# FFN gates through a DRAM scratch, and the adaLN quarters of a group in one burst: a two-layer streaming encoder

## What is computed

```python
def encoder_layer(x, c, ...):
    mod = jax.nn.silu(c) @ w_ada + b_ada
    sh1, sc1, ga1, sh2, sc2, ga2, sh3, sc3, ga3 = [m[:, None, :] for m in jnp.split(mod, 9, axis=-1)]
    h = rms_norm(x, gains[0]) * (1 + sc1) + sh1
    x = x + MACARON_W * ga1 * rms_norm(swiglu(h, w_f1_in, w_f1_out), gains[1])
    h = rms_norm(x, gains[2]) * (1 + sc2) + sh2
    y, rows = token_mixing(h, ...)
    x = x + ga2 * rms_norm(y, gains[3])
    h = rms_norm(x, gains[4]) * (1 + sc3) + sh3
    x = x + MACARON_W * ga3 * rms_norm(swiglu(h, w_f2_in, w_f2_out), gains[5])
```

## Time and profile before

| | us |
|---|---|
| median of 3 runs (1601.71 to 1602.89) | 1602.71 |
| the profiled execution | 1601.82 |
| its span in the trace | 1600.1 |
| TensorE busy | 1574.0 |
| VectorE busy | 801.3 |
| ScalarE busy | 586.7 |

### The profile page before, as it was taken

How to read it: one execution, slowest core, us unless ns; L and a number is a source line. 1 busy time by engine, 2 the same in 40 slices (tenths; PEclk the granted TensorE clock), 3 DMA queues, 4 the chain that set the end, 5 groups by cost and what they waited for, 6 DMA issues and landing times.

```text
span 1600.1 us, 26160 instructions
## 1 busy us (share of the span) xinstructions
PE 1574.0 (98%) x10238; PEld 1435.0 (90%) x10238; DVE 801.3 (50%) x1210; ACT 586.7 (37%) x814; POOL 154.2 (10%) x225
## 2 busy tenths in 40 slices
PE   5999999999999999999999999999999999999998
PEld 4999998889997899998889999987999879999987
DVE  3434442468657634443374344326675675444424
ACT  4322222264455522222272222224635554222223
POOL 5000000010342000000010000000105300000000
PEclk8999999999999999999999999999999999999999
DMA  9777744663346576444557744355534363444332
GB/s 345 249 229 219 236 132 158 210 172 106 106 137 216 174 234 193 131 131 151 182 179 227 238 130 131 131 184 183 147 108 130 105 216 106 130 131 131 132 117 81
DMA packets 254151, 266.03 MB, mean 166 GB/s; under 512 B 11727, under 2 KB 216653, under 8 KB 254066
## 3 DMA queue, kind: packets, MB, share of 16 engines
q1 hardware_dynamic: 231968, 183.52, 38.3%
q0 software_dynamic: 22080, 81.26, 14.8%
q10 hardware_dynamic: 18, 0.04, 0.0%
HBM read 258.70 MB, written 6.09 MB: 165 GB/s over the span
## 4 chain that ended last, share of the span: by engine, by line
PE 93%; DVE 3%; ACT 2%; DMA 1%; DVEq 1%; SPq 1%; issue 0%; ACTq 0%
PE ps L1984 15%; PE ps L1985 15%; PE ps L1989 15%; PE ps L2045 8%; PE ps L2047 8%; PE ps L2049 8%; PE ps L1956 4%; PE ps L1958 4%; PE ps L1957 4%; PE ps L1898 2%; DMA w_ada_g<-in_w_ada_dram 1%; PE ps L1975 1%; PE ps L1971 1%; PE ps L1972 1%; DVE x L1392 1%; PE ps L2062 1%
## 5 line engine op out<-in xcount | busy, mean ns | idle before, releaser
L1298 DVE TENSOR_TENSOR w_lo<-w_raw,w_hi 128x2048 fp32r<-128x2048 f32 x158 | 364.8, 2309 | 238.2 <-ACT w_hi L905 207.5
L1984 PE MATMUL ps<-act_hi,w_hi 128*128 128x384 f32 x1344 | 452.3, 337 | 0.0
L1985 PE MATMUL ps<-act_lo,w_hi 128*128 128x384 f32 x1344 | 449.7, 335 | 0.0
L905 ACT ACTIVATE w_hi<-w_raw 128x2048 fp32r<-128x2048 f32 x128 | 245.3, 1916 | 228.7 <-PE ps L2049 226.9
L1984 PEld LDWEIGHTS ps<-act_hi,w_hi 128*128 128x128 f32 x1344 | 252.3, 188 | 6.6 <-issue 6.6
L1985 PEld LDWEIGHTS ps<-act_lo,w_hi 128*128 128x128 f32 x1344 | 252.5, 188 | 0.0
L1989 PE MATMUL ps<-act_hi,w_lo 128*128 128x384 f32 x1344 | 246.6, 334 | 0.0
L984 ACT ACTIVATE silu_g<-ps 128x384 f32<-128x384 f32 x88 | 43.3, 492 | 537.3 <-PE ps L1989 536.5
L1989 PEld LDWEIGHTS ps<-act_hi,w_lo 128*128 128x128 f32 x1344 | 234.2, 188 | 0.0
L1459 DVE TENSOR_TENSOR hid_f<-silu_g,ps 128x384 f32<-128x384 f32 x88 | 48.8, 554 | 366.9 <-ACT silu_g L984 366.9
L2045 PE MATMUL ps<-w_hi,hid_hi 128*128 128x512 f32 x480 | 148.8, 391 | 0.0
(11 more groups left out here) (422 smaller groups left out, 1717.3 us busy)
## 6 DMA issues: line engine op xcount, KB each, us to landing
w_raw<-in_w_ffn_in_dram SPq DMA_DIRECT2D x176, 512.0 KB, 5.1
w_ada_sb<-in_w_ada_dram POOLq DMA_DIRECT2D x45, 1024.0 KB, 7.0
w_raw<-in_w_ffn_out_dram SPq DMA_DIRECT2D x88, 512.0 KB, 4.2
w_raw<-in_w_in_dram SPq DMA_DIRECT2D x46, 512.0 KB, 4.7
w_ada_g<-in_w_ada_dram POOLq DMA_DIRECT2D x16, 1024.0 KB, 5.5
w_raw<-in_w_out_dram SPq DMA_DIRECT2D x16, 512.0 KB, 5.4
w_ada_g<-in_w_ada_dram SPq DMA_DIRECT2D x5, 1024.0 KB, 15.2
w_ada_s<-in_w_ada_dram POOLq DMA_DIRECT2D x3, 1024.0 KB, 10.4
```

Of the source, the lines that this page charges most:

```text
L905: act.activation(w_hi[slot][:], w_raw[slot][:], ACT.Copy).then_inc(hi_ready.sem, 1)
L1298: dve.tensor_tensor(w_lo[slot][:], w_raw[slot][:], w_hi[slot][:].bitcast(F32), ALU.subtract).then_inc(lo_ready.sem, 1)
L1984: pe.matmul(ps[:, bank + half, 0:N], w, act_hi[:, f, :], start=(f == 0), stop=False)
L1985: pe.matmul(ps[:, bank + half, 0:N], w, act_lo[:, f, :], start=False, stop=False)
```

## The change

The two FFN gates of each layer (`nth` 0 and 2, both layers: four in all) no longer go through sixteen transposes. Behind unit 0 of the output projection one transpose (`turn_gate`) turns all 72 columns (8 chunks by 9 sequences) of the gate into a corner of PSUM bank 7. VectorE copies the 72x128 block behind the splits of units 1 and 2 (`copy_gate_rows`) to a part of `ada_rows`. POOL's queue stores it to a DRAM scratch, waits for that, and loads the two halves of `gate_tok` from it, the prompt's row broadcast to 128 partitions and each sample's row to 16 (`gates_through_dram`). VectorE waits for these loads at the head of `renorm`. The gate of the mixing part stays as it was.

The groups in the FFN input loops run their four quarters behind the fourth hidden unit. For that they have four slots, R0, R1, S0 and G4. All loads of a group wait for the last quarter of the group before, and the third and fourth also for the landing of the first and second, so that two are in flight at a time.

```diff
@@ slots
-    TWO = (R0, R1, R0, R1)
+    FOUR = (R0, R1, S0, G4)
@@ ada_loop (POOL)
+                        pool.wait_ge(ada_used, i * 4 + 4 * n0)
+                        pass_gate()
                         for q in range(4):
                             slot = ADA_SLOT[n0][q]
-                            pool.wait_ge(ada_used, i * 4 + (4 * n0 + q - 1))
-                            pass_gate()
+                            if q >= 2:
+                                earlier = ADA_SLOT[n0][q - 2]
+                                pool.wait_ge(ada_landed[earlier], i * 16 + 16 * ada_loads(4 * n0 + q - 2))
+                                pass_gate()
                             pool.dma_start(w_ada_slot[slot][:],
...
+                def gates_through_dram(n):
+
+                    pool.wait_ge(gate_rows_ready.sem, gate_rows_ready.at(l, n + 1))
+                    pass_gate()
+                    pool.dma_start(gates[l, n].rearrange("s (f n) -> f s n", n=P), gate_rows).then_inc(gate_rows_stored.sem, 16)
+                    pool.wait_ge(gate_rows_stored.sem, gate_rows_stored.at(l, n + 1))
+                    pass_gate()
+                    pool.dma_start(gate_tok[:, 1, :], gates[l, n, 1:NSEQ, :].unsqueeze(1).broadcast_to([B, S, D])).then_inc(gate_landed.sem, 16)
+                    pool.dma_start(gate_tok[:, 0, :], gates[l, n, 0:1, :].broadcast_to([P, D])).then_inc(gate_landed.sem, 16)
@@ ada_gap (POOL)
                     ada_load(m + 1, layer, components[0])
+                    gates_through_dram(gate)
                     for k, units in ((3, 3), (4, 6), (5, 8), (6, 8)):
@@ renorm (VectorE)
+                    if nth != 1:
+                        dve.wait_ge(gate_landed.sem, gate_landed.at(l, nth + 2))
@@ proj_out (VectorE)
-                    with dve.Fori(0, (units - 3) // 2) as i:
+                    split_lo(u0 + 1, (u0 + 1) % 2)
+                    split_lo(u0 + 2, u0 % 2)
+                    copy_gate_rows(nth // 2)
+                    with dve.Fori(1, (units - 1) // 2) as i:
                         for s in range(2):
                             split_lo(i * 2 + (u0 + s + 1), (u0 + s + 1) % 2)
-                    spread_gate(nth)
-                    read_gate(nth, 0)
-                    split_lo(u0 + units - 2, (u0 + units - 2) % 2)
-                    read_gate(nth, 1)
-                    split_lo(u0 + units - 1, (u0 + units - 1) % 2)
@@ four_hidden (TensorE)
                     hidden(u0, h0, norm, j, 1)
-                    pe.wait_ge(mod_ready, mods_before)
-                    quarters(range(0, 2))
                     hidden(u0, h0, norm, j, 2)
                     hidden(u0, h0, norm, j, 3)
-                    quarters(range(2, 4))
+                    pe.wait_ge(mod_ready, mods_before)
+                    quarters(range(4))
@@ turn_gate (TensorE)
+                    pe.wait_ge(gain_folded, ((FOLD_F1[0], FOLD_GAP3)[l], FOLD_GAP2[l])[n])
+                    pe.transpose(ps[0:KD * NSEQ, ADA_BANK_B, 256:256 + P],
+                                 mod[:, 6 * n + 2, :, :].rearrange("p f s -> p (f s)"), ident[:]).then_inc(gate_turned.sem, 1)
@@ proj_out (TensorE)
-                    gates_to_tokens(nth, 0)
+                    turn_gate(nth // 2)
...
-                    gates_to_tokens(nth, 1)
                     last_two(u0 + units - 2, (2 * units - 4, 2 * units - 2), hid_hi, hid_lo, nth, lambda n: None)
```

More of the change, by code:

```diff
@@ L323, in encoder_program @@
         ps = ctx.enter_context(nc.psum_tensor("ps", [P, 8, 512], F32))
+        gates = nc.dram_tensor("gate_rows_dram", (DEPTH, 2, NSEQ, D), F32, kind="Internal").ap()
+        gate_rows = ada_rows[0:KD * NSEQ, 0:P]
         def sig(name, per_layer, step=1, start=0, before=0):
@@ L382, in encoder_program @@
         FOLD_HEAD, FOLD_F1, FOLD_GAP1, FOLD_GAP2, FOLD_F2, FOLD_GAP3 = 1, (2, 7), (3, 8), (4, 9), 5, 6
-        gate_tr = sig("gate_tr", 6)
-        gate_read = sig("gate_read", 6)
-        gate_spread = sig("gate_spread", 3)
+        gate_tr = sig("gate_tr", 2)
+        gate_read = sig("gate_read", 2)
+        gate_spread = sig("gate_spread", 1)
+        gate_turned = sig("gate_turned", 2)
+        gate_rows_ready = sig("gate_rows_ready", 2)
+        gate_rows_stored = sig("gate_rows_stored", 2, 16)
+        gate_landed = sig("gate_landed", 4, 16)
         head_copied = sig("head_copied", 1)
@@ L721, in ada_loop, with ada_gap @@
                                            .rearrange("(k p) n -> p k n", p=P)).then_inc(ada_landed[slot], 16)
-                def ada_gap(n, layer, components, u0):
+                def gates_through_dram(n):
[6 more added lines that the diff above has]
+                    pool.dma_start(gate_tok[:, 0, :], gates[l, n, 0:1, :].broadcast_to([P, D])).then_inc(gate_landed.sem, 16)
+                def ada_gap(n, layer, components, u0, gate):
                     m = 4 * n
@@ L840, in _ @@
                     ada_loop(N_F2, l + 1, LOOP_F2[0], len(LOOP_F2))
-                    ada_gap(N_GAP3, l + 1, GAP_F2, U_F2OUT)
+                    ada_gap(N_GAP3, l + 1, GAP_F2, U_F2OUT, 1)
+                else:
+                    gates_through_dram(1)
             pool.wait_ge(rows_stored.sem, rows_stored.at(DEPTH, 0))
@@ L2100, in last_two @@
                     last_products(2, (0,))
-                    pe.wait_ge(gate_read.sem, gate_read.at(l, 2 * nth + 2))
+                    if nth == 1:
+                        pe.wait_ge(gate_read.sem, gate_read.at(l, 2))
+                    else:
+                        pe.wait_ge(gate_rows_ready.sem, gate_rows_ready.at(l, nth // 2 + 1))
                     banks = SAMPLE_BANKS_F2 if nth == 1 else SAMPLE_BANKS
```

45 lines of the change are left out of this document (22 added, 23 removed).

## The result

| | before | changed |
|---|---|---|
| median of 4 runs, us | 1602.21 (1601.64 to 1602.89) | 1592.88 (1592.31 to 1593.65) |
| profiled execution, us | 1601.82 | 1593.65 |
| its span, us | 1600.1 | 1592.1 |

The changed kernel takes 0.9942 of the time, 95% interval 0.993 to 0.9953: 9.3 us less, by the interval 7.5 to 11.2. The forecast was 1593.4 from a sum of -9.3.

What follows compares the result with a forecast made beforehand. TensorE's stream was taken to bound the kernel: -7.1 (transpose groups) + 0.7 (lone transposes) - 2.9 (burst edges) = -9.3 us, from 1602.71 to 1593.4 us, range 1590.5 to 1597.5.

Steps and rivals of the forecast that it cites:

- What bounds the kernel: Whole span: TensorE, 98% busy, runs end to end outside the start; VectorE and ScalarE count only where it would wait.
- Eight groups at 0.89: FFN output projections: removing eight groups of eight transposes, 0.89 us each, takes 7.1 us off the path.
- The lone transpose at 0.17: FFN output projections: one gate transpose in each of four adds 0.7 us in all, bounds 0.4 and 3.6.
- a dear lone transpose: Rival, FFN output projections: a lone transpose costs like a whole group, 0.89 us, giving 1596.3; chance 5 in 100.
- transposes that do not overlap: Rival, FFN output projections: each transpose costs its full 0.273 us, giving 1583.4 with the bursts; chance 1 in 100.
- The gates' path costs nothing: Copy, store and loads of the FFN gates: 12 us long, landed near 270, hidden by 49 us of cover.
- May slip by a few us: Load of the gap's fourth quarter, behind POOL's two new waits: a few us late at no cost, needed only near 328.8.
- Bursts at 0.36 per edge: FFN input loops: merging eight pairs of bursts saves the two edges of a burst, 0.36 us each time, 2.9 in all.
- The upper bound from the weight queue's idle time: FFN input loops: merging saves 0.67 us each, 5.4 in all, if all idle time at a burst went.
- A burst does not starve the weights: Weight loads behind a burst of four quarters: at most 19 us to land, so TensorE never waits; nothing charged.
- the 20 of the prediction: Weight loads behind a burst: one may take 20 us to land before TensorE waits.
- What would show it: Signs in the changed profile: group period 37.3 us, one burst of 3.8, TensorE's waits unchanged, VectorE not waiting for gate loads.

Runs made afterwards that it cites:

- gates_only: The kernel before with only the FFN gates moved through DRAM, the groups keeping two bursts of two quarters: 1596.14 us, ratio 0.9961.
- eight_turns: The changed kernel with the gate's one transpose issued eight times over, same output: 1596.74 us, ratio 0.9964.
- late_gates: The changed kernel with the gate turned, stored and loaded only from ahead of the projection's last two units, so without cover: 1622.01 us, ratio 1.012.
- three_bursts: The changed kernel with three bursts per group, of one, one and two quarters, loads and slots unchanged: 1598.24 us, ratio 0.9976.
- bursts_only: The kernel before with only the bursts merged (four slots, new load pacing), the gates keeping their transposes: 1599.28 us, ratio 0.9981.
- again: The changed kernel timed and profiled once more, nothing altered: 1592.75 us, ratio 0.9941.
- third_gate: The changed kernel with the mixing part's gate also sent through DRAM, loaded near 495 us: 1608.24 us, ratio 1.0031.
- extra_traffic: The changed kernel plus two unread 512 KB loads per layer into DRAM scratch, behind the second unit of the mixer's output projection: 1593.12 us, ratio 0.9944.

## Why the prediction was right, point by point

**What bounds the kernel.** Right: behind the start TensorE's busy time fell by 9.4 us, transposes and edges together, and the span by 9.2; VectorE's 11.5 us were worth nothing by themselves.

**Eight groups at 0.89.** Right: gates_only gave -6.1 where the two terms give -7.1 + 0.5 = -6.6; eight_turns shows 0.89 for eight again.

**The lone transpose at 0.17.** High by 0.05: it costs 0.12, the lower bound of 0.11 being nearer than the row that was taken. In the sum this is 0.2 us. The rival of a dear lone transpose is out. So is the rival of transposes that do not overlap: 28 more of them cost 3.5 us in eight_turns, where it had 7.6. The figure of the Trainium skill, "TensorE: Matmul & The Clock Gate", "Part 4: PE-mode transpose", about 275 ns for a 128x128 one in bf16, is again the duration (0.27 for L2076), and again not the spacing.

**The gates' path costs nothing.** Right in the outcome, with wrong inputs. The copy was put one unit too late: the two splits written ahead of the loop are those of units 1 and 2, and the second starts at 246.28, not near 255.6. The loads took 7.2 and 9.0 us, not 5.3, and the path is 15.7 us long here and 17.3 in late_gates, not 12. The two errors work against each other: the cover was 54 us, not 49. So none of this mattered, and late_gates shows the price without it, which is not the path's length either: 9 us for each of the first three renormalisations and 1.4 for the last. "May slip by a few us" for the fourth quarter's load: it did not slip.

The write's completion, of which "DMA: Bandwidth & Descriptors", "Anatomy of one DMA", in the Trainium skill warns, took 4.5 us for 36 KB here, less than a load of that size. Its rule in "Rules for kernel authors" on an outermost dimension of 8 is neither shown nor excluded by any run. The samples' load, which has that dimension, took 6.1 to 7.2 us over the program, and the prompt's row, spread to 128 partitions, 8.0 to 9.0; but the second is issued 0.6 us behind the first, and the times do not tell how many engines each used.

**Bursts at 0.36 per edge.** Right: 0.36 by the period of a group, 0.34 by three_bursts, -3.0 us by bursts_only. The upper bound from the weight queue's idle time was rightly not taken.

**A burst does not starve the weights.** Right: 10.5 us behind a paced burst and 15.5 behind an unpaced one are under the 20 of the prediction. Its 7.1 was the median of a pair, whose second load, the one that counts, took 7.6, so the same working gives 19.6; no run went past that, and the limit itself is not shown. What the prediction did not mention is the start: there one split waited for its weights for 3.0 us (4.7 in again; the longest such wait before was 1.5, at another split), and TensorE did not wait.

```profile
57.06 1.92 ACT L928 ACTIVATE w_hi<-w_raw 128x2048 fp32r<-128x2048 f32 x1 [3.01 <-DMA w_raw<-in_w_ffn_in_dram]
```

**What would show it.** The period (37.33), the burst (3.82), the list of waits and the free VectorE came as said. From the lone transpose to the place of the former second group it is 65.4 us (243.90 to 309.31), where 65.5 was said.

**Sum.** -7.1 + 0.5 - 2.9 = -9.5 with the measured transpose, against -9.3 and -9.5 in two sets of runs and -9.2 by the profiles. The mechanism is shown term by term. That the medians meet the forecast within 0.5 us is in part luck: their interval is about 2 us to either side, and the forecast started from 1602.71, the median of three runs, where four gave 1602.21.

## What to carry to other kernels

In a stream that one engine bounds, price a small operation by the starts of its neighbours with and without it, not by its duration: 273 ns in the duration column were 0.11 us of time. Count the switches between kinds of work beside the work, since merging two bursts is free if the loads can be kept flowing. A detour through DRAM is free only under cover: ask how long the path is (16 to 17 us here), how early its input exists, and also whose loads are in flight while it runs, for in a stretch where the queues are full a third such detour cost 14 us more than it saved.

## What the runs showed of the hardware

- While loads that spread a few DRAM rows over 128 partitions were in flight, the DMA engines moved 128 to 229 GB/s at 90% busy or more in most slices (third_gate, 501 to 506 us; 139 to 213 in the changed kernel near 260). With adaLN's and the output weights' loads they moved some 400 (extra_traffic, 500 to 502), and with the FFN input weights' alone, whose runs are 128 floats, some 290 (515 to 520). The same bytes from DRAM to DRAM cost no time (1593.1).
- The switch from products with 128-wide weights to the narrow adaLN ones and back costs 0.35 us per burst, whatever the burst's length (one, two or four quarters took 1.21, 2.09 and 3.82).
- A transpose of 72 columns costs what one of 128 costs: 0.89 us for eight.
- TensorE waits of 7 to 8 us brought a lower granted clock, towards their end and for some 5 us behind them: in late_gates 1.00 in the first 3 us of the wait and 0.50 in the 4 us behind it, and in third_gate 0.68 over the 16 us that hold the wait (519 to 535). A wait of 7.3 us cost 9.2.
